# Experts of a gated network: gathering and the preceding expert's return moved between the last two units' down products, the return in two rounded passes, three places for picks

## What is computed

```python
def moe_swiglu(x, router_w, w1, w3, w2):
    t = x.reshape(B * S, D)                      # 256 x 1024
    logits = (t @ router_w).astype(jnp.float32)
    top_v, top_i = lax.top_k(logits, TOP_K)      # 2 of 8
    gates = jax.nn.softmax(top_v, axis=-1)
    combine = jnp.sum(jax.nn.one_hot(top_i, N_EXPERTS) * gates[..., None], axis=1)
    out = jnp.zeros_like(t)
    for e in range(N_EXPERTS):                   # w1, w3: 1024 x 3584, w2: 3584 x 1024
        out = out + combine[:, e:e + 1] * swiglu(t, w1[e], w3[e], w2[e])
    return out.reshape(B, S, D)

def swiglu(x, w1, w3, w2):
    return (jax.nn.silu(x @ w1) * (x @ w3)) @ w2
```

## Time and profile before

| | |
|---|---|
| median of 3 runs | 2405.87 us (2404.7 to 2407.78) |
| profiled execution | 2408.15 us, its span 2406.0 us |
| TensorE busy | 2189.7 us, 91% of the span |
| VectorE, ScalarE, GpSimd busy | 58%, 47%, 53% |
| expert stage | about 805 to 2008 us of the span |

### The profile page before, as it was taken

The page is one execution under the profiler, slowest core; times in us unless marked ns, Lnnn a source line. Parts: engine busy times, 40 slices in busy tenths (PEclk is TensorE's granted clock), DMA queues, the critical chain, the costliest instruction groups (busy, mean ns, idle before and its releaser), DMA issues.

```text
span 2406.0 us, 26806 instructions
## 1 busy us (share of the span) xinstructions
PE 2189.7 (91%) x10576; PEld 1743.8 (72%) x10576; DVE 1407.4 (58%) x1744; ACT 1141.1 (47%) x1156; POOL 1286.9 (53%) x555
## 2 busy tenths in 40 slices
PE   8988699989888699999999999999899996887997
PEld 7577488865675577777777777888677773746997
DVE  1774533345744576777767676343367675455665
ACT  1143234321431475766667674333366672534554
POOL 0334145402440497988989796455389892204453
PEclk9999899989999799999999999999999998978999
DMA  8210075523000598999989897455489894204550
GB/s 293 105 36 1 16 257 181 181 97 130 36 1 1 202 367 310 340 338 323 368 294 368 294 362 261 174 180 195 156 288 363 296 366 146 105 35 158 210 193 35
DMA packets 208105, 485.11 MB, mean 202 GB/s; under 512 B 9168, under 2 KB 13008, under 8 KB 206928
## 3 DMA queue, kind: packets, MB, share of 16 engines
q1 hardware_dynamic: 207952, 483.02, 55.6%
HBM read 481.96 MB, written 1.05 MB: 201 GB/s over the span
## 4 chain that ended last, share of the span: by engine, by line
PE 82%; DVE 11%; ACT 3%; issue 2%; SPq 1%; DMA 1%; POOL 0%; DVEq 0%; ACTq 0%
PE bank L920 20%; PE bank L922 19%; PE bank L921 19%; PE bank L549 11%; PE bank L741 5%; PE bank L556 3%; DVE b_arena L1244 2%; DVE b_arena L1238 1%; DVE e_lo L1696 1%; PE bank L1016 1%; PE bank L702 1%; ACT e_hi L2050 1%; DVE b_X L1238 1%; PE bank L1131 1%; DVE b_arena L1241 1%
## 5 line engine op out<-in xcount | busy, mean ns | idle before, releaser
L2655 POOL TENSOR_TENSOR e_lo<-b_ring,e_hi 128x512 fp32r<-128x512 f32 (+3 forms) x407 | 1135.0, 2811 | 594.1 <-ACT e_hi L2050 594.1
L1696 DVE TENSOR_TENSOR e_lo<-b_ring,e_hi 128x1536 fp32r<-128x1536 f32 (+1 forms) x403 | 770.1, 1912 | 483.3 <-ACT e_hi L2050 479.2
L2050 ACT ACTIVATE e_hi<-b_ring 128x2048 fp32r<-128x2048 f32 (+1 forms) x407 | 776.5, 1911 | 396.0 <-PE bank L922 358.4
L920 PE MATMUL bank<-e_hi,e_xh 128*128 128x512 f32 (+1 forms) x1200 | 481.4, 401 | 35.4 <-issue 25.1
L922 PE MATMUL bank<-e_hi,e_xl 128*128 128x512 f32 (+1 forms) x1200 | 469.0, 391 | 0.0
L921 PE MATMUL bank<-e_lo,e_xh 128*128 128x512 f32 (+1 forms) x1200 | 468.7, 391 | 0.0
L920 PEld LDWEIGHTS bank<-e_hi,e_xh 128*128 128x128 f32 x1200 | 228.2, 190 | 103.8 <-issue 55.6
L920 PE MATMUL bank<-e_hi,e_th 128*128 128x512 f32 x688 | 271.4, 394 | 2.4 <-DVE e_tl L1700 2.4
L922 PE MATMUL bank<-e_hi,e_tl 128*128 128x512 f32 x688 | 268.4, 390 | 0.0
L921 PE MATMUL bank<-e_lo,e_th 128*128 128x512 f32 x688 | 268.2, 390 | 0.0
L922 PEld LDWEIGHTS bank<-e_hi,e_xl 128*128 128x128 f32 x1200 | 228.1, 190 | 48.5
(11 more groups left out here) (211 smaller groups left out, 2413.2 us busy)
## 6 DMA issues: line engine op xcount, KB each, us to landing
b_ring<-in_moe_w SPq DMA_DIRECT2D x168, 2048.0 KB, 8.2
b_ring<-in_w_in SPq DMA_DIRECT2D x15, 2048.0 KB, 9.1
b_ring<-in_ffn_w SPq DMA_DIRECT2D x15, 2048.0 KB, 7.8
b_ring<-in_w_up SPq DMA_DIRECT2D x12, 2048.0 KB, 8.0
b_ring<-in_w_down SPq DMA_DIRECT2D x6, 2048.0 KB, 9.2
b_ring<-in_w_o SPq DMA_DIRECT2D x4, 2048.0 KB, 7.9
b_gain<-in_gains SPq DMA_DIRECT2D x7, 1024.0 KB, 4.8
b_ring<-in_w_out SPq DMA_DIRECT2D x2, 2048.0 KB, 8.4
```

The source lines that it names most:

```text
L920: e.matmul(out, ah, bh, start=first, stop=False)
L1696: e.tensor_tensor(lo[:, 0:at], raw[:, 0:at], r32(hi[:, 0:at]), ALU.subtract).then_inc(lo_dve.sem)
L2050: return e.activation(out, x, ACT.Copy)
L2655: e.tensor_tensor(lo[:, at:], raw[:, at:], r32(hi[:, at:]), ALU.subtract).then_inc(lo_pool.sem)
```

## The change

The order of the steps: for one tile, T of unit 6 now stands between the two d pieces of unit 5; behind the second of them come the gathering for the next expert, into banks 0 and 2, and the return of the preceding expert, into banks 6, 7, 1 and 3; then d of unit 6. For two tiles the order of the list stays, but TensorE turns h of the first tile before it makes the second tile's last d product of unit 5. Turned h of one-tile experts alternates between two buffers, and gathered x between the two blocks.

The return: the shares leave the matrices. `e_G` and `e_GT` are dropped, and the picks are turned instead, behind T of unit 4 for one tile, with two tiny products that bring the gate of each place into a column (`turn_picks`). ScalarE multiplies d's two halves by the gate and rounds them to `e_yh`, VectorE makes the rest `e_yl`, and the return is picks times `e_yh` plus picks times `e_yl` in rounded passes, eight instead of four fp32 products. Since returns are later now, three places hold turned picks and gates. The second tile's return stays in fp32. VectorE's `selected` moves from unit 5's to unit 1's T and behind it, and `add_back` of one-tile experts moves behind the split of d of unit 6. The first two pieces of an expert are split 6 to 2 like the others.

```diff
-def steps_of(widths):
+def steps_of(widths, tiles):
     out, n = [], len(widths)
     for u in range(n + 1):
-        out += [("w1", u, 0)] * (u < n) + [("T", u - 1, 0)] * (u > 0)
+        out += [("w1", u, 0)] * (u < n) + [("T", u - 1, 0)] * (0 < u < n)
         if u < n:
             out += [("w1", u, 1), ("w3", u, 0), ("w3", u, 1)]
         if u:
-            out += [("d", u - 1, h) for h in range(widths[u - 1] // 256)]
+            down = [("d", u - 1, h) for h in range(widths[u - 1] // 256)]
+            if u == n - 1:
+                down.insert(1 if tiles == 1 else len(down), ("T", u, 0))
+            out += down
...
+            e_yh, e_yl = eb("yh", [128, 1024], F32R), eb("yl", [128, 1024], F32R)
+            e_PT = [[eb(f"PT{i}", [128, 256], F32R) for i in range(3)], [eb("PTb", [128, 256])]]
+            e_gate = [[eb(f"gate{i}", [128, 8]) for i in range(3)], [eb("gateb", [128, 8])]]
...
# TensorE
+                            if tiles == 2 and u == n - 2 and hf == 1:
+                                turn_h(s, n - 1)
...
-            def turn_shares(ex, s, b):
-                turn(bank[b], [e_G[s][:, t, :] for t in range(2)]).then_inc(gt_turn[s].sem)
+            def turn_picks(ex, s, b):
+                e.wait_ge(*pick[s](ex))
+                turn(bank[b], [e_P[s][:, t, :] for t in range(2)])
+                sums(bank[b][:, 256:257], [(e_P[s][:, t, :], comb[:, t, ex:ex + 1]) for t in range(2)]).then_inc(pt_turn[s].sem)
+            def finish(ex, banks):
+                e.wait_ge(*y_dve[0](ex))
+                e.wait_ge(*y_act[0](ex))
+                if ex:
+                    e.wait_ge(*acc_add[0](ex - 1))
+                pt = e_PT[0][ex % 3]
                 for t in range(2):
                     for n in range(2):
-                        e.matmul(bank[first + 2 * t + n][:, :], gt[:, tok(t)], y[n], start=True, stop=True).then_inc(back[s].sem)
+                        b = bank[banks[2 * t + n]]
+                        e.matmul(b[:, :], pt[:, tok(t)], e_yh[:, half(n)], start=True, stop=False)
+                        e.matmul(b[:, :], pt[:, tok(t)], e_yl[:, half(n)], start=False, stop=True).then_inc(back[0].sem)
...
+                def aside(kind, u, hf):
+                    if ex and tiles == 2 and (kind, u, hf) == ("w1", 0, 1):
+                        finish(ex - 1, (4, 5, 6, 7))
+                    if more and tiles == 1 and kind == "T" and u == 4:
+                        if ex > 1:
+                            e.wait_ge(*acc_add[0](ex - 2))
+                        turn_picks(ex + 1, 0, 6)
+                    if tiles == 1 and (kind, u, hf) == ("d", 5, 1):
+                        if more:
+                            gather(ex + 1, 0, 0, 0)
+                            e.wait_ge(*tl_out(unit + 6))
+                            gather(ex + 1, 0, 1, 2)
+                        if ex:
+                            if more:
+                                e.wait_ge(*pt_out[0](ex + 1))
+                            finish(ex - 1, (6, 7, 1, 3))
...
# VectorE
-                    if p + 2 < ends:
-                        split_rest(p + 2, 4 if tail and p + 2 >= at + 42 else 6)
-                    if add_last and (kind, u, hf) == ("w3", 0, 0):
-                        add_last()
+                        if p + 2 < ends:
+                            split_rest(p + 2, 6)
...
-                    ts(e_P[s][:, t, :], j, r, None, ALU.is_equal)
-                    ins = ts(e_G[s][:, t, :], j, r, comb[:, t, ex:ex + 1], ALU.is_equal, ALU.mult)
+                    ins = ts(e_P[s][:, t, :], C("iota")[:, 128 * s:128 * s + 128], rank[:, t, ex:ex + 1], None, ALU.is_equal)
...
+                e.tensor_copy(e_PT[s][k][:, :], bank[b][:, 0:256])
+                e.tensor_copy(e_gate[s][k][:, 0:1], bank[b][:, 256:257]).then_inc(pt_out[s].sem)
...
+                    if more and kind == "T" and u == 1:
+                        selected(ex + 1, 0)
+                    if more and tiles == 1 and (kind, u, hf) == ("d", 5, 1):
+                        for g in range(2):
+                            gathered(ex + 1, 0, g, 2 * g)
+                    if ex and tiles == 1 and (kind, u, hf) == ("d", 6, 0):
+                        add_back(ex - 1, 0, (6, 7, 1, 3))
+                    if more and tiles == 1 and (kind, u, hf) == ("w3", 5, 0):
+                        picks(ex + 1, 0, 6)
...
-                e.tensor_copy(e_y[:, half(0)], bank[4][:, :]).then_inc(y_dve[0].sem)
+                e.wait_ge(*pt_out[0](ex))
+                for n in range(2):
+                    e.wait_ge(*y_act[0](ex, n))
+                    stt(e_yl[:, half(n)], bank[4 + n][:, :], e_gate[0][ex % 3][:, 0:1], r32(e_yh[:, half(n)]),
+                        ALU.mult, ALU.subtract).then_inc(y_dve[0].sem)
...
# ScalarE
+                e.wait_ge(*pt_out[0](ex))
+                if ex:
+                    e.wait_ge(*back[0](ex - 1))
+                for n in range(2):
+                    f(e_yh[:, half(n)], bank[4 + n][:, :], ACT.Copy, 0.0, e_gate[0][ex % 3][:, 0:1]).then_inc(y_act[0].sem)
                 if tiles == 2:
-                    copy(e_h[1][:, :], bank[7][:, :]).then_inc(y_act[1].sem)
-                copy(e_y[:, half(1)], bank[5][:, :]).then_inc(y_act[0].sem)
+                    e.wait_ge(*pt_out[1](ex))
+                    f(e_h[1][:, :], bank[7][:, :], ACT.Copy, 0.0, e_gate[1][0][:, 0:1]).then_inc(y_act[1].sem)
...
# GpSimd
-                    split_rest(MOE_P + 42 * ex + i, 4 if ex and i < 2 else 6)
+                    split_rest(MOE_P + 42 * ex + i, 6)
```

246 lines of the change are left out of this document (137 added, 109 removed).

## The result

| | before | after |
|---|---|---|
| median of the timed runs | 2406.82 us (4 runs, 2404.7 to 2410.18) | 2394.89 us (4 runs, 2391.86 to 2396.64) |
| ratio, with 95% interval | | 0.9948 [0.9931, 0.9965] |
| span of the profiled execution | 2406.0 us | 2394.7 us |
| expert stage, first product of expert 0 to the end of the last down product | 817.42 to 2002.61: 1185.2 us | 816.07 to 1991.52: 1175.5 us |

The change saves 12 us, 0.5%. The direction was forecast and the time lies in the range, 3.6 us under the forecast of 2398.5. Of the 11.3 us between the two spans 9.7 lie in the expert stage and 1.35 ahead of it.

What follows compares the result with a forecast made beforehand. The prediction took TensorE, busy 91% of the span, to bound the kernel. Its terms, -10.5 -3.5 -2.4 +2.1 +3.4 +1.2 +2.5 = -7.2 us, took the 2405.87 us median to about 2398.5 us, range 2389 to 2407.

Steps and rivals of the forecast that it cites:

- The return, -10.5: Seven returns on TensorE: eight rounded passes take 1.94 us instead of 3.44, saving 1.5 us each, 10.5 in all.
- The rival that passes wouldn't be cheaper: Rounded return passes run like fp32's, so returns save nothing to 0.4 us each: 2406.4 to 2409 us; chance 0.05.
- The selection, -3.5: VectorE's selection moved from unit 6 to unit 1 shortens TensorE's stall, 0.6 us for each of six experts.
- The last turn of h, -2.4: Earlier turns in expert 7's unit 6 and the first layer's gated network remove TensorE waits, 1.6 to 2.4 us.
- Turned picks, +2.1: Behind unit 4's turn, added gate passes cost 0.2 us for each of six experts, 0.45 twice for the two-tile one.
- The seam, +3.4: Between experts, VectorE's added work delays TensorE: +0.5 us at four seams, +0.35 at the first, +1.0 out of expert 5.
- TensorE resumes at E+3.1: At a seam, TensorE restarts 3.1 us after its last product's end (E), instead of 2.4 to 2.7, following VectorE's products.
- The rival "the branch sets the seam": Instruction fetch after the branch sets the seams, so the seam and clock charges fall away: 2394 us; chance 0.20.
- The first unit, +1.2: An expert's first unit loses the pause the old return gave the splitters: 0.2 us for six experts, at most 0.7.
- The clock, +2.5: Longer idle at seams brings two more 3.4 us stretches at 1.2 GHz, 1.25 us each.
- Given back: Rival: slow stretches at all seams and the far end of the first unit give 2405.3 us; chance 0.18.
- The rival "slower": The expert's end becomes VectorE's: six seams grow by 2.2 us instead of 0.5, 2414 us; chance 0.07.

Runs made afterwards that it cites:

- e1: Changed kernel with the return again four true fp32 products at its new place, the rest e_yl left out; 2407.09 us, ratio 0.9997.
- e9: Kernel before with only the return made in eight rounded passes at its old place; 2390.65 us, ratio 0.9921.
- e4: Kernel before with only VectorE's selection for the next expert moved from unit 5 to unit 1; 2403.63 us, ratio 0.9985.
- e12: Kernel before with the rounded return of e9, the moved selection of e4 and an early tiny silu on ScalarE; 2389.81 us, ratio 0.9922.
- e8: Changed kernel without the tiny gate-column products in experts 1 to 4 and 7 and expert 5's first tile; 2389.68 us, ratio 0.9926.
- e10: Changed kernel with 64 idle TensorE instructions, an early tiny silu and the second tile's half of d first in ScalarE's order; 2386.18 us, ratio 0.9906.
- e5: Changed kernel with 128 idle TensorE instructions ahead of the first gathering; 2398.10 us, ratio 0.9961.
- e3: Changed kernel with 64 idle TensorE instructions ahead of the first gathering; 2388.82 us, ratio 0.9923.
- e7: Kernel before with 64 idle TensorE instructions ahead of its first gathering; 2405.32 us, ratio 0.9994.
- e6: Changed kernel with 192 idle TensorE instructions ahead of the first gathering; 2408.42 us, ratio 1.0000.
- e2: Changed kernel with VectorE raising the counter for the next expert ahead of its two products of y; 2394.61 us, ratio 0.9946.

## Why the prediction was right and where it failed

The forecast's terms were for the profiled execution; after's, span to span, is 11.3 us shorter, where they summed to 7.2. Most of the forecast saving, the return, was right by its mechanism. That the total came within 3.6 us of the measured time is in part luck: the terms of the seam and the clock were 6.3 us too high together, for reasons that did not hold, and those of the picks and the first units 2.6 too low.

**The return, -10.5: right.** 1.91 us for eight passes against the 1.94 forecast and 3.44 before, 1.53 saved seven times, 10.7. e1 pays it back, e9 gets it alone. In the table's last column the rounding is worth 11.3 (e1 against after) and 11.5 (e9 against before), where seven times 1.53 are 10.7 and seven times the 1.64 of the old place are 11.5. The rival that passes wouldn't be cheaper is out. At the end the return of expert 7 has a wait of 2.37 us instead of 0.83, as its two steps on each engine suggested, and then runs its passes at 0.43 us, at the lower clock. From the last down product's end to the return's it takes 5.84 us instead of 4.50. In e9, at full clock, it takes 4.22, so "nothing" was right but for the clock:

```profile
1993.88 0.76 PE L1053 MATMUL bank<-e_yh,e_PT 128*128 128x512 f32 x1 [2.37 <-DVE e_yl L1309]
1994.45 0.63 PE L1054 MATMUL bank<-e_yl,e_PT 128*128 128x512 f32 x1
1994.87 0.63 PE L1053 MATMUL bank<-e_yh,e_PT 128*128 128x512 f32 x1
```

**The selection, -3.5: right.** From the turn at unit 5 to the next one were 15.15 us for five pieces. In after there are four pieces and 11.77 us (the turn of unit 6 is at 1196.06); with a piece of 2.72 that is 14.49, so 0.66 saved against the 0.6 forecast. The cover in unit 1 held in after (17.31 to 17.34 us from the turn of unit 1 to the next), while e4 and e12, whose selection has two instructions more, lose about 0.2 of their 0.57 there.

**The last turn of h, -2.4: right.** The 1.64 us in expert 7 and the 0.81 us in the first layer are gone.

**Turned picks, +2.1: too low.** I took 0.2 us for each expert, because the stall ahead of w3 would absorb half of what is added. TensorE in order of time, unit 4 of expert 2 and the turn of unit 5:

```profile
1166.32 0.60 PE L574 MATMUL bank<-b_cst,e_h 128*128 128x128 f32 x4
1166.76 0.38 PE L574 MATMUL bank<-b_cst,e_P 128*128 128x128 f32 x2
1166.98 0.50 PE L567 MATMUL bank<-b_moe_comb,e_P 128*128 128x1 f32 x4
1167.34 0.48 PE L938 MATMUL bank<-e_hi,e_xh 128*128 128x512 f32 x1
...
1184.29 0.60 PE L574 MATMUL bank<-b_cst,e_h 128*128 128x128 f32 x4
```

Turn to turn 17.97 us instead of 17.31: 0.66 more, less the 0.22 of two transposes that the tail no longer has. So 0.44, the full price of the added passes; e8 gets its 0.40 back in full. The stall moved and absorbed nothing. For six experts 2.6 instead of 1.2.

**The seam, +3.4: wrong in mechanism and sign.** The sum of the seven seams from 947 us on went from 25.75 to 24.33 us, -1.4. The five between one-tile experts, with the stop at 1214.82, grew by 1.9 us (12.79 to 14.71), not far from the 2.35 forecast but for another reason; the two at expert 5 fell by 3.3 (4.48 to 3.22 into it, 8.48 to 6.40 out of it), where the forecast had no change. The last of these is code and partly chance: it is 5.57 to 8.08 us in the runs with after's order. The step that failed is "TensorE resumes at E+3.1": the timing of VectorE was right within 0.4 us, but TensorE waits for counters that go up once ScalarE's second step is done (1344.58 in this seam, E+0.43 in before's) and for code, whichever comes last, not for the product. Only the +1.0 out of expert 5 held: the second return waits 2.03 instead of 0.99 us, for ScalarE's e_h, and e10 takes it back by the order of ScalarE's steps. The rival "the branch sets the seam", whose 2394 us is what was measured, had this part of the mechanism; but it left all seams as they were, where after has 1.80 and 4.40.

**The first unit, +1.2: somewhat low.** From first product to turn of unit 0 after's experts 2 and 4 take 15.73 us with one slow stretch, expert 7 14.13 without one; before, 17.18 less the return's 3.44 is 13.74. That is 0.4 each, 2.4 for six; the far end was 0.7. A gap of 0.28 us stands ahead of w1 of unit 1:

```profile
1093.73 0.39 PE L940 MATMUL bank<-e_hi,e_xl 128*128 128x512 f32 x1
1094.23 0.47 PE L938 MATMUL bank<-e_hi,e_xh 128*128 128x512 f32 x1
```

**The clock, +2.5: wrong in count and in price.** After has nine slow stretches in the stage, as before (7.9 and 7.3 of them in work), though two seams between one-tile experts are over 3 us. And one costs 1.6 us, not 1.25: I had it from the distance of two experts' starts, which contains two different seams. From start to turn, as above the table, it is clean. This term should have had 0 and a spread of several stretches either way at 1.6; e5, with after's work, has four.

**The sum with what was measured:** -10.7 for the returns, -4.0 for the selection, -2.4 for the last turn, +2.6 for the picks and 0.9 for those of the two-tile expert as forecast, +2.4 for the first units, -1.4 and +1.0 for the seams and 0 for the clock are -11.6, against -11.3 span to span; by the slow stretches in work the clock is +1.0 and the sum -10.6. So the forecast was 3.8 us too high at the seams and 2.5 at the clock, 0.7 at the returns and the selection, and 2.6 too low at the picks and the first units.

**Given back** was a rival at 2405.3. For the moves alone it is what happened: e1 keeps them all and stands at 0.9997. In the table's columns, before to e1: idle -7.3 (6.3 of them the waits for e_tl), rest +7.2. Six times 0.66 for the picks, 0.4 for the first unit and -0.17 for the tail (from the turn of unit 5 to E, without return and stall, 24.07 instead of 24.24 us) are 5.3 of these 7.2. The forecast had the moves at +3.3 us together, seams and clock among them. That they come to about nothing instead is the seams and the clock, against dearer picks and first units.

**Two sums of the prediction** don't come out, and nothing hangs on them. The rival "slower" gives -12.1 + 13.2 + 6.3 = +7.4, so 2413 us and not 2414, and with all stretches slow it is slower than before from 1.0 us a seam, not 0.8. Seven returns of sixteen times 0.23 us are 1.7 us more than seven of 3.44; it is 2.4 only with 0.1 for each edge.

**What stays open.** Why the first transfer of code begins 1.1 us ahead of E in some seams and behind it in others, and why TensorE needs the second before it can start in the seam of 4.40 us and not in the others; that this goes with the place of the code is shown by e3, e5 and e8 only together with small shifts in time. Why the seam behind expert 0 stays at 3.3 to 3.7 us in all of after's variants. What decides whether a seam is followed by a slow stretch: 4.40 us of idle time were followed by one of them, 2.70 by two, 2.44 by none and 1.80 (at 1344.65) by one. Whether e9 with after's order of T and d, but without the gate products, would beat e10 was not tried.

## What to carry to other kernels

Price each part of a change alone: here a rounding of ten lines was worth all of it, and the reordering around it, with three places and a new order on four engines, returned what it took. Where an engine branches, look for the transfers of instructions in the DMA view before you blame a semaphore, since a gap marked "issue" that changes when nothing near it was edited can be a matter of code layout; measure it once with idle instructions ahead of the loop. And compare stages, not totals, when the effect is a few microseconds, and take the slow stretches in work out of them: the unchanged code ahead of the stage came out up to 4 us apart between profiles, and 5.4 of the 5.6 us by which e9's stage beats after's are the clock.

## What the runs showed of the hardware

- Counter increments that stand behind a VectorE instruction pass once what that instruction waits for is there; they don't wait for its start or its end. In before they passed 0.87 us ahead of the copy's start (1079.08 against 1079.95); in after TensorE went on 0.61 us before the product's end, at 1344.65 against 1345.26.
- A transfer of instructions on q8 (16 KB: the page has 101 with 1.65 MB) takes 0.9 to 1.4 us at the seams between after's one-tile experts. Where TensorE waits for it, its next product comes 1.3 to 1.9 us behind the transfer's end in before and after (once 2.6 in e7). A seam between two one-tile experts is 1.80 us where the first transfer starts 1.1 to 1.35 us ahead of the last product's end, 2.4 to 2.7 where it starts 0.14 to 0.36 ahead, 3.35 where it starts 0.49 behind, and 4.40 where TensorE stands until a second one, 2.02 behind, has come.
- A counter increment in TensorE's own queue costs about 0.155 us (64 more between e5 and e6: 9.9 us).
- A stretch of 3.4 us at the 1.2 GHz level costs 1.6 us of dense products, and nothing as far as it falls into a gap: with only the part in work counted, after, e2, e3, e5 and e6 agree in the rest within 0.5 us.
- A true fp32 product of 128x128 by 512 takes 0.86 us, edges included (3.44 for four), two rounded passes 0.48 (1.91 for four pairs).
